# Mixer end of a two-layer trunk: small loads on ScalarE's queue, slab in halves, last tile without GpSimd, two expert tiles issued early

## The reference

```
h = x
for i in range(2):
    a = rms_norm(h, norm_mix[i])
    h = h + (even_mixer(a) if i == 0 else odd_mixer(a))     # attention heads | S5 and gated DeltaNet; both end in o @ w_out
    h = h + hier_moe(rms_norm(h, norm_ffn[i]))              # one group of 4, two experts of 8 in it, FF 512, weights normalized
    h = h + sigmoid(rms_norm(h, ple_norm[i]) @ w_g + b_g) * (p[i] @ w_p)
```

## Time and profile before

| | us |
|---|---|
| median of 3 runs | 2957.79 |
| lowest, highest | 2955.67, 2961.13 |
| the profiled execution | 2960.23 |
| its span in the profile | 2958.6 |
| mean granted clock of TensorE in it | 0.977 |

### The profile page before, as it was taken

How to read it: one execution, slowest core, us unless ns; L and a number is a source line. 1 busy time by engine, 2 the same in 40 slices (tenths; PEclk the granted TensorE clock), 3 DMA queues, 4 the chain that set the end, 5 groups by cost and what they waited for, 6 DMA issues and landing times. The chain is left out here.

```text
span 2958.6 us, 41299 instructions
## 1 busy us (share of the span) xinstructions
PE 2760.8 (93%) x16673; PEld 1417.6 (48%) x16674; DVE 1090.9 (37%) x2394; ACT 674.3 (23%) x1312; POOL 229.4 (8%) x288
## 2 busy tenths in 40 slices
PE   8999999999999999999989899988999989999998
PEld 5544555555543233334457744488655323232344
DVE  3585455553510000004456635555563000000053
ACT  3310354541110000002420123333211000000132
POOL 0000000000100000002000000055211000000020
PEclk9999999999999999999999999999999999999999
DMA  4000693006399999997110120000517999999931
GB/s 167 29 29 0 244 408 116 1 19 233 127 344 409 412 409 411 409 414 278 43 47 29 17 72 29 0 3 25 200 57 266 387 408 409 406 413 404 392 129 43
DMA packets 139127, 609.40 MB, mean 206 GB/s; under 512 B 27780, under 2 KB 34340, under 8 KB 122536
## 3 DMA queue, kind: packets, MB, share of 16 engines
q1 hardware_dynamic: 115976, 529.59, 45.7%
q0 software_dynamic: 15296, 53.49, 4.9%
q10 hardware_dynamic: 7664, 23.66, 2.1%
HBM read 503.81 MB, written 101.71 MB: 205 GB/s over the span
## 5 line engine op out<-in xcount | busy, mean ns | idle before, releaser
L2857 PE MATMUL acc<-xt,work 128*128 128x512 f32 x384 | 166.9, 593 | 0.0
L695 PE MATMUL acc<-h,xt 128*128 128x512 f32 x384 | 165.2, 592 | 0.0
L328 PE MATMUL scores<-xt 65*128 65x512 f32 (+7 forms) x384 | 146.0, 489 | 0.4 <-DVE xt L469 0.4
L1768 PE MATMUL pu<-place 128*32 128x512 f32 (+2 forms) x912 | 141.4, 628 | 0.6 <-issue 0.6
L1768 PE MATMUL py<-place 128*32 128x512 f32 (+2 forms) x672 | 126.5, 615 | 12.5 <-issue 12.4
L1768 PE MATMUL pg<-place 128*32 128x512 f32 (+1 forms) x528 | 130.4, 594 | 0.0
L475 DVE TENSOR_REDUCE nmax<-scores 128x1 f32<-128x256 f32 (+7 forms) x128 | 96.8, 757 | 73.9 <-PE scores L330 71.8
L1252 PE MATMUL acc<-place 128*128 128x512 f32 x256 | 118.0, 605 | 2.5 <-DMA place<-in_ev_w_out_dram 1.4
L695 PEld LDWEIGHTS acc<-h,xt 128*128 128x128 f32 x384 | 72.9, 190 | 91.1 <-issue 90.9
L2857 PEld LDWEIGHTS acc<-xt,work 128*128 128x128 f32 x384 | 72.0, 190 | 86.1 <-issue 86.1
L1863 DVE COPY work<-py 128x512 f32<-128x512 f32 x21 | 14.5, 692 | 226.6 <-PE py L1768 226.6
(11 more groups left out here) (755 smaller groups left out, 5467.1 us busy)
## 6 DMA issues: line engine op xcount, KB each, us to landing
place<-in_moe_w_up_dram SPq DMA_DIRECT2D x25, 2048.0 KB, 25.7
slots_out<-zeros SPq DMA_DIRECT2D x4, 9216.0 KB, 63.0
place<-in_moe_w_down_dram SPq DMA_DIRECT2D x18, 2048.0 KB, 25.8
xt<-in_moe_w_up_dram SPq DMA_DIRECT2D x17, 2048.0 KB, 25.3
xt<-in_moe_w_gate_dram SPq DMA_DIRECT2D x16, 2048.0 KB, 23.9
place<-in_moe_w_gate_dram SPq DMA_DIRECT2D x16, 2048.0 KB, 23.4
xt<-in_moe_w_down_dram SPq DMA_DIRECT2D x15, 2048.0 KB, 27.6
s_t<-in_moe_w_gate_dram SPq DMA_DIRECT2D x10, 2048.0 KB, 24.3
```

What stands on the lines that cost most here:

```text
L328: pe.matmul(bank(n, u)[:, a * SLAB:a * SLAB + w], qkt[0:kind(p).rows, p % 2, u, 0, i * P:(i + 1) * P], qkt[0:kind(p).rows, p % 2, u, 1, a ...
L695: last = pe.matmul(acc[:, n % 4, 0:width], xs[:, k, tile_of(i)], weights[:, k, cols], start=(k == 0), stop=(k == k_of - 1))
L1768: last = pe.matmul(out[part], lhs[:, k, part], weights_of(kind, q)[:, k, cols], start=(k == 0), stop=(k == k_last), skip_group_check=True)
L2857: last = pe.matmul(acc[:, n % 4, :], slabs[m // 4 % 2][:, k, (m % 4) * P:(m % 4 + 1) * P], xt[:, k, half * SLAB:(half + 1) * SLAB], start= ...
```

## The change

1. The slab is loaded in two halves (k 0 to 3, k 4 to 7) with a semaphore each; the second half is waited for at the fifth matmul.
2. The six small loads (gains, gain_col, w_group, w_expert, biases) move from SP's queue to ScalarE's, at the start of its part, in layer 1 behind `root_o(0)` and `copy_o(0)`. SP issues the preloads right behind the residuals.
3. The squares' full-size result goes into a PSUM bank `junk`; the wait for the scatter moves to VectorE's `scale(i)`.
4. The last tile: VectorE multiplies h by the gains in two halves (`gain_last`), ScalarE scales the result in place by 1/rms, GpSimd's multiply goes.
5. In layer 1 `turn_o(0)` moves behind the first four matmuls.
6. `keep_busy` 24 becomes 16, and 10 becomes 5.
7. Row 3 of the table is written first; SP then reads two expert numbers and issues tiles 6 and 7 in `mixer_end`, behind the first rows. The experts' stage starts its own issues at tile 8.

The core of the diff:

```diff
@@ -1207,19 +1209,12 @@
     def _(sp):
-        with nc.allow_non_contiguous_dma(reason="router weights, short rows, column slabs"):
-            for tile, view in slab_loads:
-                sp.dma_start(tile, view).then_inc(z["slabs_in"], 16)
-            sp.dma_start(h[:, 0:2], residual.rearrange("(t p) d -> p t d", p=P)[:, 0:2]).then_inc(residual_in[0], 16)
-            for n in range(1, 4):
-                two = slice(2 * n, 2 * n + 2)
-                sp.dma_start(h[:, two], residual.rearrange("(t p) d -> p t d", p=P)[:, two]).then_inc(residual_in[n], 16)
-            sp.dma_start(gains, row(t["norm_ffn"][layer]).to_broadcast([P, D])).then_inc(z["gain_in"], 16)
-            sp.dma_start(gain_col[:], t["norm_ffn"][layer].rearrange("(k p) -> p k", p=P)).then_inc(z["router_in"], 16)
-            sp.dma_start(w[:, :, 0:GROUPS], t["moe_w_group"][layer].rearrange("(k p) n -> p k n", p=P)).then_inc(z["router_in"], 16)
-            sp.dma_start(w[:, :, GROUPS:ROUTES], t["moe_w_expert"][layer].rearrange("(k p) n -> p k n", p=P)).then_inc(z["router_in"], 16)
-            sp.dma_start(bias[:, 0:GROUPS], row(t["moe_b_group"][layer]).to_broadcast([P, GROUPS])).then_inc(z["router_in"], 16)
-            sp.dma_start(bias[:, GROUPS:ROUTES], row(t["moe_b_expert"][layer]).to_broadcast([P, EXPERTS])).then_inc(z["router_in"], 16)
+        with nc.allow_non_contiguous_dma(reason="column slabs"):
+            sp.dma_start(slabs[1][:, 0:4], last_slab[:, 0:4]).then_inc(z["slab_head_in"], 16)
+            sp.dma_start(slabs[1][:, 4:8], last_slab[:, 4:8]).then_inc(z["slab_tail_in"], 16)
+        for n in range(4):
+            two = slice(2 * n, 2 * n + 2)
+            sp.dma_start(h[:, two], residual.rearrange("(t p) d -> p t d", p=P)[:, two]).then_inc(residual_in[n], 16)
         for n, (tile, view) in enumerate(own_loads):
             if n >= early_loads:
                 sp.wait_ge(z["products"], 2 * NT - 1 if n == early_loads else 2 * NT)
@@ -1229,6 +1224,11 @@
             sp.wait_ge(scattered[n], c.scattered_before[n])
         for n in range(2):
             sp.dma_start(first_rows[:, n, :], c.slots_in[n * REGION:n * REGION + P, :]).then_inc(c.first_in[n], 16)
+        views = expert_weights(t, layer)
+        sp.wait_ge(z["listed"], 1)
+        for n, (tile, kind, q) in enumerate(listed_loads):
+            expert = sp.value_load(r.table[0:1, 3, q:q + 1], min_val=0, max_val=EXPERTS - 1)
+            sp.dma_start(tile, views[kind][expert]).then_inc(c.listed_in[n], 16)
         sp.wait_ge(z["own_in"], 16 * len(own_loads))
@@ -1244,8 +1244,10 @@
                 pe.wait_ge(z["added"], 2 * (i - 1) + n + 1)
-            if i == 0 and n == 1 and ks[0] == 0 and slab_loads:
-                pe.wait_ge(z["slabs_in"], 16 * len(slab_loads))
+            if i == 0 and n == 1 and ks[0] == 0:
+                pe.wait_ge(z["slab_head_in"], 16)
+            if i == 0 and n == 1 and ks[0] == 4:
+                pe.wait_ge(z["slab_tail_in"], 16)
             if delta is not None and n == 0 and ks[0] == KD // 2:
@@ -1278,12 +1280,12 @@
 
-        if delta is not None:
-            turn_o(0)
         for i in range(NT):
             product(i, 0, range(0, 4))
             if i:
                 turn(i - 1, 1)
+            elif delta is not None:
+                turn_o(0)
             product(i, 0, range(4, KD))
@@ -1300,7 +1302,7 @@
         score(NT - 1, 1)
-        keep_busy(pe, c, o_bank, 24)
+        keep_busy(pe, c, o_bank, 16)
         rank_tokens(NT - 1)
@@ -1314,7 +1316,7 @@
         pe.matmul(turned[:, 1, EXPERTS:2 * EXPERTS], over_wide, earlier, start=True, stop=True).then_inc(z["spread_out"], 1)
-        keep_busy(pe, c, o_bank, 10)
+        keep_busy(pe, c, o_bank, 5)
 
@@ -1337,9 +1339,9 @@
             act.wait_ge(z["added"], 2 * i + n + 1)
-            if n == 0 and i >= RING_M:
-                act.wait_ge(scattered[i % RING_M], before[i % RING_M] + 32 * (i // RING_M))
-            act.activation(m[:, i % RING_M, half], h[:, i, half], ACT.Square, scale=1.0 / math.sqrt(D), accum_out=half_ms[:, i, n:n + 1]).then_inc(z["squares"], 1)
+            if 2 * i + n:
+                act.wait_ge(z["squares"], 2 * i + n)
+            act.activation(junk[:], h[:, i, half], ACT.Square, scale=1.0 / math.sqrt(D), accum_out=half_ms[:, i, n:n + 1]).then_inc(z["squares"], 1)
 
@@ -1348,6 +1350,13 @@
             copy_o(0)
+        with nc.allow_non_contiguous_dma(reason="router weights, short rows"):
+            act.dma_start(gains, row(t["norm_ffn"][layer]).to_broadcast([P, D])).then_inc(z["gain_in"], 16)
+            act.dma_start(gain_col[:], t["norm_ffn"][layer].rearrange("(k p) -> p k", p=P)).then_inc(z["router_in"], 16)
+            act.dma_start(w[:, :, 0:GROUPS], t["moe_w_group"][layer].rearrange("(k p) n -> p k n", p=P)).then_inc(z["router_in"], 16)
+            act.dma_start(w[:, :, GROUPS:ROUTES], t["moe_w_expert"][layer].rearrange("(k p) n -> p k n", p=P)).then_inc(z["router_in"], 16)
+            act.dma_start(bias[:, 0:GROUPS], row(t["moe_b_group"][layer]).to_broadcast([P, GROUPS])).then_inc(z["router_in"], 16)
+            act.dma_start(bias[:, GROUPS:ROUTES], row(t["moe_b_expert"][layer]).to_broadcast([P, EXPERTS])).then_inc(z["router_in"], 16)
         for i in range(NT):
@@ -1357,8 +1366,9 @@
             root(i)
+        act.wait_ge(z["gained"], 2)
         act.wait_ge(z["rstd_made"], NT)
-        act.activation(m[:, (NT - 1) % RING_M, :], h[:, NT - 1, :], ACT.Copy, scale=rstd[:, NT - 1:NT]).then_inc(z["normed"], 1)
+        act.activation(m[:, (NT - 1) % RING_M, :], m[:, (NT - 1) % RING_M, :], ACT.Copy, scale=rstd[:, NT - 1:NT]).then_inc(z["normed"], 1)
         act.wait_ge(z["shifted"], 1)
@@ -1392,9 +1402,18 @@
 
+        def gain_last(n):
+            i, half = NT - 1, slice(n * SLAB, (n + 1) * SLAB)
+            if n == 0:
+                dve.wait_ge(scattered[i % RING_M], before[i % RING_M] + 32 * (i // RING_M))
+            dve.wait_ge(z["added"], 2 * i + n + 1)
+            dve.tensor_tensor(m[:, i % RING_M, half], h[:, i, half], gains[:, half], ALU.mult).then_inc(z["gained"], 1)
+
         def scale(i):
             if i == 0:
                 dve.wait_ge(z["gain_in"], 16)
+            if i >= RING_M:
+                dve.wait_ge(scattered[i % RING_M], before[i % RING_M] + 32 * (i // RING_M))
             dve.scalar_tensor_tensor(out=m[:, i % RING_M, :], in0=h[:, i, :], scalar=rstd[:, i:i + 1], in1=gains[:],
@@ -1464,10 +1483,14 @@
             add(i, 0)
+            if i == NT - 1:
+                gain_last(0)
             if i:
                 choose(i - 1)
                 place(i - 1)
             add(i, 1)
+            if i == NT - 1:
+                gain_last(1)
             if i < NT - 1:
@@ -1477,7 +1500,7 @@
         place(NT - 1)
-        dve.wait_ge(z["scaled"], NT)
+        dve.wait_ge(z["gained"], 2)
 
@@ -1507,8 +1530,8 @@
         dve.wait_ge(z["tabled"], 1)
+        dve.tensor_copy(r.table[:, 3, E], acc[0:1, 1, EXPERTS:2 * EXPERTS]).then_inc(z["listed"], 1)
         step(dve.tensor_copy(over, acc[0:1, 1, E]))
-        step(dve.tensor_copy(r.table[:, 3, E], acc[0:1, 1, EXPERTS:2 * EXPERTS]))
         step(dve.scalar_tensor_tensor(out=starts, in0=acc[0:1, 1, EXPERTS:2 * EXPERTS], scalar=float(REGION), in1=cap_at[0:1, :],
@@ -1539,8 +1562,6 @@
                 pool.wait_ge(z["normed"], 1)
-                pool.tensor_tensor(m[:, i % RING_M, :], m[:, i % RING_M, :], gains[:], ALU.mult).then_inc(z["scaled"], 1)
-                pool.wait_ge(z["scaled"], NT)
             pool.wait_ge(z["placed"], i + 1)
@@ -1703,15 +1724,17 @@
             n = at_tile[kind, part.q]
-            if n >= preloaded:
-                pe.wait_ge(tile_in[places[n]], 16 * places[preloaded:n + 1].count(places[n]))
+            if n >= preloaded + LISTED:
+                pe.wait_ge(tile_in[places[n]], 16 * places[preloaded + LISTED:n + 1].count(places[n]))
+            elif n >= preloaded:
+                pe.wait_ge(c.listed_in[n - preloaded], 16 * (layer + 1))
 
     last_expert = {}
 
     @block.sync
     def _(sp):
         expert = {}
-        for n in range(preloaded, len(tiles)):
+        for n in range(preloaded + LISTED, len(tiles)):
             kind, q = tiles[n]
@@ -1929,6 +1952,14 @@
     for n, (kind, q) in enumerate(tiles[0:EARLY])]
+
+
+def listed(ring):
+
+
+    _, units = expert_units()
+    tiles, places, _ = weight_order(units)
+    return [(ring[places[n]].rearrange("p (k n) -> p k n", k=FF // P if tiles[n][0] == 2 else KD), *tiles[n]) for n in range(EARLY, EARLY + LISTED)]
 
```

More of the change, by code:

```diff
@@ L1042, in even_mixer @@
         ring = own + [flat_fk, s5_t.rearrange("p k n -> p (k n)"), flat_fv] + behind
-        mixer_end(nc, c, t, layer, h, t["x"][0], lambda k, i: mixed_t[k][:, i], slabs, [(slabs[1], slab_of(t["ev_w_out"][j], SLAB))], m, normed, mt, spare,
-                  preloads(t, layer, ring), 4, r, ch, gains=gains)
```

(9 more changed lines are left out.)

7 lines of the change are left out of this document (4 added, 3 removed).

## The result

The changed kernel takes 3001.54 us in the median of 4 runs (2999.40 to 3005.31), the kernel before 2959.46 in the same comparison (4 runs, 2955.67 to 2962.87). The ratio is 1.0144, 95% interval 1.0126 to 1.0162: slower by 42 us, where +34 was forecast.

What follows compares the result with a forecast made beforehand. TensorE, busy 93%, was taken as the bound, with full DMA engines in the expert stage. Heads 18.1 + 16 and tail and seam 0 gave 34 on 2960.2, less 2.4 for the median: 2992 us, range 2947 to 3002.

Steps and rivals of the forecast that it cites:

- Rows share one for one: Queues sharing a DMA engine pass one row each per turn, whatever its size; layer 0's first scores come 18.1 us later.
- the term of 16 for layer 1's head: Layer 1, first products to first scores: 16 us later, the middle of 10.3 and 21.3.
- ScalarE free at once: Layer 1's head: issues do not hold ScalarE, scores +10.3 us; as a rival 2986, inside the forecast's chance of 0.58.
- ScalarE held: Layer 1's head: ScalarE held by its issues until some 1400 rows are left, tile 0's turn 21.3 us later.
- the clock behind a long wait: Lower TensorE clock after idling: priced only at the seam to the experts, within 3.3 us in layer 0, 0.9 in layer 1.
- Tail and seam: Last tile to experts: -2.2 + 3.3 in layer 0, -2.2 + 0.9 in layer 1, together 0, lower bound -4.3 us.
- An expert stage that starts a microsecond later ends a microsecond later: Expert stage: TensorE and DMA engines have no room, so a later start delays the end by about as much.
- rival 2: Rows pass in bunches, no clock fall at the seam: 10.6 us gained at most, 2947 to 2951; chance 0.18.
- `turn_o`: Layer 1's head: moving it behind four matmuls gains up to 3.6 us if residual 0 and ScalarE are not late.
- The argument from the skill's packets: Heads: with packets of 9 to 17 descriptors, 216 rows take 13 to 24 turns and the heads' terms vanish.
- Signs: Profile marks expected: equal queue counts, w_group's ScalarE issue over 5 us, add(0,0) after 2130, group_eq 0.22, first expert product 8 to 9.
- The range's upper end of 3002: Whole kernel: slowest time allowed, in the forecast's own range of 2984 to 3002 and the full range from 2947.

Runs made afterwards that it cites:

- run 1: Changed kernel with the six small loads back on SP's queue, between residuals and preloads: 2960.90 us, ratio 1.0000.
- run 2: Kernel before the change with only the six small loads moved to ScalarE's queue: 3001.80 us, ratio 1.0136.
- run 3: Changed kernel with SP's preloads held until the router's loads are in: 2970.18 us, ratio 1.0032.
- run 4: Changed kernel with the small loads, still on ScalarE's queue, in 1152 rows instead of 3456, same bytes: 2970.28 us, ratio 1.0033.
- run 7: Kernel of run 5 with keep_busy back at 24 and 10 rounds: 2956.27 us, ratio 0.9987.
- run 8: Last tile's multiply back on GpSimd, on the kernel of run 7: 2955.81 us, ratio 0.9988; on that of run 10: 2951.91 us, ratio 0.9977.
- run 10: Kernel of run 5 with the block-end filler at 10 rounds in layer 0, 17 in layer 1: 2953.30 us; also without listed tiles: 2951.82 us.
- run 9: Kernel of run 7 with layer 1's turn_o(0) ahead of the first products again: 2958.62 us, ratio 1.0001.
- run 5: Changed kernel with the small loads back on SP's queue and in 1152 rows instead of 3456: 2953.02 us, ratio 0.9981.

## Where the prediction held, and the step that failed

- **Rows share one for one: right**, shown by the counts 1221 to 1221 and by runs 1 to 4. First scores of layer 0 at 703.52, forecast 702.5 to 703: +18.67, forecast +18.1. That it is so near has some luck in it: 698.7 + 2.5 + 0.5 is 701.7, which is +16.9, and nothing is given for the other 1.2.
- **The step that failed is the term of 16 for layer 1's head.** The mechanism was right and the value too small. The sum took the middle of 10.3 (ScalarE free at once) and 21.3 (ScalarE held), with the reason that SP's held issue was seen under other traffic. The runs show no half way: ScalarE was held until 33.2 us after the block's start (forecast for the held case: 35), and the first turn came 19.5 us later than before, counted from the block's start. The router's loads were in at 37 us, as forecast (2137 is 36.9), but they did not set the time, since the held ScalarE came first in the chain. ScalarE was free with 1884 rows of its queue still to pass, where some 1400 were assumed.
- **A second term was put at nothing: the clock behind a long wait.** After the 17.6 us wait of layer 0 the scores take 3.63 instead of 2.02, which with what follows makes +1.55 until the last scores; in layer 1 the first turn and product at the lower clock add 1.65 until the first scores. Together 3.2 us. The granted clock is 0.50 from 703.52 to 707 and from 2157.6 to 2160; the prediction priced the lower clock only at the seam.
- **Tail and seam: 0 forecast, -0.7 and -0.2 found**, with both opposite terms near their prices: 2.17 for `group_eq` (0.22 again) and 2.7 for the lower clock in layer 0, forecast 3.3. The filler of 24 rounds had no price in the sum; it was a bound of its own once the stall was gone (run 7).
- **"An expert stage that starts a microsecond later ends a microsecond later": holds for the 19.5 us of layer 0 (19.7 at the last turn), roughly for layer 1 (43.3 becomes 40.5), and not for one or two** (runs 8 and 10). That sentence made the gains of rival 2 too large: even with both heads free of stalls and the fillers fitted, the kernel is 7 to 8 us faster than before by the medians, 6 to 8 by the ratios, not the 10.6 of that rival's sum.
- **`turn_o`: up to 3.6 forecast, 3.7 found, but taken up by the router** in the kernel with the small loads on SP's queue (run 1), kept where the router is early (run 9).
- **The argument from the skill's packets was wrong, though the rule it set aside did not hold here.** The prediction says that with packets of 9 to 17 descriptors the head's terms would vanish. That follows only if SP's queue sends one row in its turn. If both queues send as many rows in a turn, 216 small rows still stand against 216 large ones, however long the turns are.
- **Signs.** The long issue on ScalarE was not w_group's (0.67 and 3.45 us, over 5 forecast) but w_expert's and the bias's behind it (8.25 and 15.30 in layer 0, 16.81 and 7.30 in layer 1). The other signs came: equal counts, `add(0,0)` after 2130 (2156.89), `group_eq` at 0.22, the first expert product at 9.01. The range's upper end of 3002 is given without a sum, and the measured 3001.54 lies half a microsecond below it.
- The sum of terms was 34, the medians show 42. The profiled executions show 38.9; of it 18.7 + 1.5 and 19.5 + 1.6 are heads and clock, -0.9 tails and seams, and the remaining -1.5 is the sum of the experts' stages, the stretch between the layers and the end, which the sum put at nothing.

What stays open: whether the skill's packets of several descriptors exist for other forms of load; no run here had one. The slab in halves and the squares' new target were tested by no run of their own; run 1 shows only that they, with the rest of the change, sum to nothing. And single-microsecond effects in the experts' stage are below what 11 runs tell apart.

## What to carry to other kernels

Count rows, not bytes, before a small load gets a queue of its own: beside a queue full of large rows each of its rows costs one large row's time (router +18.7 us), while behind the large rows on their own queue 1900 such rows passed in a microsecond. An engine that has work to do should not issue more rows than its queue takes at once, since it stands still until enough of them have drained. And a wait removed is worth only the distance to the next late thing: lay out the small load in long rows first, then move the turn forward.

## What was not expected of the hardware

A bias load of 2 KB held ScalarE for 15.30 us, longer than the load of 128 KB ahead of it (8.25), while the rows issued ahead of it drained. A transpose that reads every fourth column of h is hardly dearer than one of neighbouring columns: 283 ns against 274 in the mean of 56 in layer 0 (run 5 against before), and first to last scores take 113.8 us there against 113.2 in run 3, which reads neighbouring columns and has the same clock there. VectorE's stall beside GpSimd's multiply is not bound to one operation: 2.39 on `group_eq` before, 2.02 on the operation two later in run 8. Both end within 0.03 us of the multiply.
